# A two-layer-stack transformer kernel: the residual kept feature-major instead of token-major

## The reference

```python
# layers 0 and 1
for i in range(2):
    x = x + 0.5 * swiglu(rmsnorm(x, ffn1_norm[i]), gate[i], up[i], down[i])
    h = rmsnorm(x, mix_norm[i])             # gated linear attention (i=0), latent attention (i=1)
    o_mem = memory_cross_attention(q_mem, rmsnorm(mem, mem_norm[i]), mem_w_kv[i], ...)
    x = x + concat([o, o_mem]) @ w_out[i]
    x = x + 0.5 * swiglu(rmsnorm(x, ffn2_norm[i]), ...)
# layers 2 and 3
for i in range(2):
    h = rms_norm(x, g_mix_pre[i])           # grouped-query attention, and attention into mem_2
    x = x + rms_norm(concat([tok, mo]) @ w_o[i], g_mix_post[i])
    h = rms_norm(x, g_ffn_pre[i])
    x = x + rms_norm((silu(h @ w_gate) * (h @ w_up)) @ w_down, g_ffn_post[i])
```

## Time and profile before

| | |
|---|---|
| median of the runs | 1841.42 us (1838.01 to 1844.0, 3 runs) |
| profiled execution | span 1837.2 us (the page has no time around it) |
| PE | 1718.0 us busy, 94% |
| DVE | 1095.9 us, 60% |
| ACT | 899.6 us, 49% |
| POOL | 76.6 us, 4% |
| moved | 289.20 MB, mean 157 GB/s |
| L1675 to L1677 (gate, up) | 2112 matmuls of 256 columns each |
| L1706 (down) | 3 x 528 of 512 columns |
| L1609 (row products, out and memory too) | 3 x 514 |

### The profile page before, as it was taken

The page is one execution under the profiler, slowest core; times in us unless marked ns, Lnnn a source line. Parts: engine busy times, 40 slices in busy tenths (PEclk is TensorE's granted clock), DMA queues, the critical chain, the costliest instruction groups (busy, mean ns, idle before and its releaser), DMA issues.

```text
span 1837.2 us, 29340 instructions
## 1 busy us (share of the span) xinstructions
PE 1718.0 (94%) x10778; PEld 1516.3 (83%) x10778; DVE 1095.9 (60%) x1613; ACT 899.6 (49%) x1430; POOL 76.6 (4%) x99
## 2 busy tenths in 40 slices
PE   7999999889999999999799999996899998889998
PEld 6999887579999899987678999873699986579997
DVE  4555666455555655567765555558565556755554
ACT  5444453445444544445555444456544444754443
POOL 1000000000000100001201000000100000110000
PEclk9999999999999999999899999999999998999999
DMA  6655444245555455545224555550255553145553
GB/s 210 194 192 183 162 148 138 92 160 161 188 183 187 149 184 185 182 158 184 80 96 155 190 184 186 170 174 1 97 201 193 179 184 107 47 138 190 185 185 114
DMA packets 79654, 289.20 MB, mean 157 GB/s; under 512 B 8928, under 2 KB 9184, under 8 KB 79216
## 3 DMA queue, kind: packets, MB, share of 16 engines
q1 hardware_dynamic: 78272, 282.23, 46.4%
q0 software_dynamic: 1008, 5.24, 0.8%
q10 hardware_dynamic: 320, 1.01, 0.2%
HBM read 287.39 MB, written 1.05 MB: 157 GB/s over the span
## 4 chain that ended last, share of the span: by engine, by line
PE 81%; DVE 9%; ACT 5%; issue 2%; DMA 2%; POOL 1%; SPq 0%; DVEq 0%; ACTq 0%
PE ps L1706 18%; PE ps L1609 16%; PE ps L1677 13%; PE ps L1675 13%; PE ps L1676 13%; DVE wlo L981 2%; PE ps L1555 2%; PE ps L1937 2%; PE ps L1901 1%; DMA raw<-units 1%; ACT whi L637 1%; DVE inv L1476 1%; DVE act_lo L992 1%; ACT junk L660 1%; ACT act_hi L648 1%
## 5 line engine op out<-in xcount | busy, mean ns | idle before, releaser
L1675 PE MATMUL ps<-act_hi,whi 128*128 128x256 f32 x2112 | 603.1, 286 | 4.0 <-DVE wlo L981 3.1
L1676 PE MATMUL ps<-act_lo,whi 128*128 128x256 f32 x2112 | 599.8, 284 | 0.0
L1677 PE MATMUL ps<-act_hi,wlo 128*128 128x256 f32 x2112 | 599.7, 284 | 0.0
L1157 DVE TENSOR_TENSOR wlo<-raw,whi 128x1024 fp32r<-128x1024 f32 x358 | 437.0, 1221 | 177.9 <-ACT whi L777 177.7
L1675 PEld LDWEIGHTS ps<-act_hi,whi 128*128 128x128 f32 x2112 | 407.4, 193 | 10.9 <-DVE wlo L981 3.7
L777 ACT ACTIVATE whi<-raw 128x1024 fp32r<-128x1024 f32 x358 | 365.7, 1052 | 101.9 <-DMA raw<-units 100.9
L1676 PEld LDWEIGHTS ps<-act_lo,whi 128*128 128x128 f32 x2112 | 407.4, 193 | 4.7
L1677 PEld LDWEIGHTS ps<-act_hi,wlo 128*128 128x128 f32 x2112 | 407.2, 193 | 0.0
L981 DVE TENSOR_TENSOR wlo<-raw,whi 128x1024 fp32r<-128x1024 f32 x176 | 211.9, 1226 | 116.0 <-ACT whi L637 115.5
L1126 DVE TENSOR_TENSOR prob<-ps,prob 128x512 f32<-128x512 f32 x132 | 91.3, 692 | 252.8 <-PE ps L1677 252.6
L637 ACT ACTIVATE whi<-raw 128x1024 fp32r<-128x1024 f32 x176 | 180.9, 1055 | 119.2 <-DMA raw<-units 114.1
(11 more groups left out here) (187 smaller groups left out, 1522.2 us busy)
## 6 DMA issues: line engine op xcount, KB each, us to landing
raw<-units SPq DMA_DIRECT2D x534, 512.0 KB, 3.4
arena<-mem_in POOLq DMA_DIRECT2D x3, 1024.0 KB, 6.8
gpost<-post_in POOLq DMA_DIRECT2D x4, 512.0 KB, 4.8
x<-x_in SPq DMA_DIRECT2D x2, 512.0 KB, 4.6
out<-x SPq DMA_DIRECT2D x2, 512.0 KB, 3.2
const<-const_in ACTq DMA_DIRECT2D x1, 816.0 KB, 4.5
row<-row_in ACTq DMA_DIRECT2D x1, 134.0 KB, 5.1
const<-const_in SPq DMA_DIRECT2D x1, 64.0 KB, 3.0
```

What stands on the lines that cost most here:

```text
L1157: V.tensor_tensor(wlo[:, u % RING, :], raw[:, u % RAW, :], whi[:, u % RING, :].bitcast(F32), ALU.subtract).then_inc(lo_ready, 1)
L1675: T.matmul(out_, whi[:, slot, w], act_hi[:, k, :], start=k == 0, stop=False)
L1676: T.matmul(out_, whi[:, slot, w], act_lo[:, k, :], start=False, stop=False)
L1677: ins = T.matmul(out_, wlo[:, slot, w], act_hi[:, k, :], start=False, stop=k == KD - 1)
```

## The change

- `x`, memory and the output lie with features on partitions (8 tiles of 128 features x 256 tokens). The host turns x, mem and mem_2 before and the output after. No transposes of x or of memory are left; those of keys, queries and probabilities stay.
- Down and out (`sum_unit`): the weight tile is stationary and the hidden chunk or the heads move, 256 columns, 8 output tiles x 3 passes per unit. In the last unit each of the four banks is reported when it is done (`sum_done`), and DVE adds it to x at once (`x_ready` now counts banks).
- The order inside an FFN: down is two chunks behind gate/up instead of one. In the first chunk PE runs all high passes of gate and up first (`norm_hi`), then the low ones (`norm_lo`). Banks 6 and 7 hold the first two chunks. `LEAD` is 4.
- Sum of squares: ACT squares x by banks of 128x512 into `sq`; POOL adds them (`folded`, three adds of 512 columns and one of 256) to `fold`, 256 columns; PE multiplies that by a column of ones (`columns_of_fold`), which gives one sum per token; DVE makes the mean, POOL the root, DVE the diagonal (was POOL), PE spreads it, DVE copies it. `columns_of_fold` stands in PE's list after the third unit of an FFN, `spread` after the fourth. At a post end DVE does the adds.
- Beside memory x is multiplied with the root by POOL (`normed`, four of 128x512). At a post end ACT applies the gain from PSUM (`gained`), DVE multiplies by the spread root and adds, bank by bank. `gpost` and its four loads are gone.
- Loads at the start: gain first, x in four parts with unit 0 between them, the identity behind them; memory is loaded in four parts later.

```diff
-RAW, RING, LEAD = 3, 6, 3
+RAW, RING, LEAD = 3, 6, 4
...
+                def folded(self, slot, first=True):
+                    for b in range(BANKS):
+                        pool.wait_ge(square_ready, self.squares + b + 1)
+                        if b > 0:
+                            if b > 1:
+                                pool.wait_ge(pool_step, self.steps)
+                            nc.gpsimd.tensor_tensor(sq[:, 0], sq[:, 0], sq[:, b], ALU.add).then_inc(pool_step, 1)
+                            self.steps += 1
+                    pool.wait_ge(pool_step, self.steps)
+                    nc.gpsimd.tensor_tensor(fold[:, slot, :], sq[:, 0, 0:S], sq[:, 0, S:2 * S], ALU.add
+                                            ).then_inc(fold_ready, 1)
...
+                def bank_squares(self, src, here):
+                    if self.folds:
+                        act.wait_ge(fold_ready, self.folds)
+                    self.folds += 1
+                    for b in range(BANKS):
+                        here(b)
+                        nc.scalar.activation(sq[:, b], src(b), ACT.Square).then_inc(square_ready, 1)
...
+                        for b in range(1, BANKS):
+                            dve.wait_ge(square_ready, self.squares + b + 1)
+                            self.step(V.tensor_tensor(sq[:, 0], sq[:, 0], sq[:, b], ALU.add))
+                        V.tensor_tensor(fold[:, 0, :], sq[:, 0, 0:S], sq[:, 0, S:2 * S], ALU.add
+                                        ).then_inc(fold_ready, 1)
+                        self.mean(end, 5)
+                        self.diagonal(end)
+                        self.spread(5)
+                        for b in range(BANKS):
+                            dve.wait_ge(gained, self.gains_)
+                            self.step(V.tensor_tensor(o, o, doubled(inv_rms), ALU.mult))
+                            V.tensor_tensor(bank_of(x, b), bank_of(x, b), post_x[:, b], ALU.add).then_inc(x_ready, 1)
...
+                def columns_of_fold(self, slot, bank):
+                    pe.wait_ge(fold_ready, self.folds)
+                    for t in range(TT):
+                        ins = T.matmul(ps[:, bank, t:t + 1], fold[:, slot, t * P:(t + 1) * P], ones[:, 0:1],
+                                       start=True, stop=True)
+                    ins.then_inc(cols_done, 1)
...
+                def sum_unit(self, k, slot, hi, lo, first, last):
+                    for b in range(BANKS):
+                        for d in range(2):
+                            w = slice((2 * b + d) * P, (2 * b + d + 1) * P)
+                            o = ps[:, b, d * S:(d + 1) * S]
+                            T.matmul(o, wlo[:, slot, w], hi, start=first and d == 0, stop=False)
+                            T.matmul(o, whi[:, slot, w], hi, start=False, stop=False)
+                            ins = T.matmul(o, whi[:, slot, w], lo, start=False, stop=last and d == 1)
+                        if last and b < BANKS - 1:
+                            ins.then_inc(sum_done, 1)
+                    ins.then_inc(unit_used, 1)
...
+                    first_chunk()
+                    gate(1, U0 + 2, 0)
+                    self.columns_of_fold(0, 5)
+                    up(1, U0 + 3, 0)
+                    self.spread(5)
+                    gate(2, U0 + 4, 0)
+                    up(2, U0 + 5, 0)
+                    down(0, 0, first=True)
+                    pe.wait_ge(inv_ready, self.diags)
+                    gate(3, U0 + 7, 0)
+                    up(3, U0 + 8, 0)
+                    down(1, 0)
+                    with pe.Fori(0, (CH - 4) // 2) as i:
+                        for c in (4, 5):
+                            pe.wait_ge(scaled_ready, i * 2 + (gu + c - 1))
+                            gate(c, U0 + 3 * c - 2, i)
+                            up(c, U0 + 3 * c - 1, i)
+                            down(c - 2, i)
```

More of the change, by code:

```diff
@@ L215, in ffn @@
             down = self.w["w_down_2"][n]
-        for c in range(CH + 1):
+        for c in range(CH + 2):
             if c < CH:
@@ L303, in build @@
         gate_up_rms = prob[:, 2:4]
-        gpost = sb("gpost", [P, D])
+        flat_rows = rows[:].rearrange("p t n -> p (t n)")
+        sq = flat_rows.rearrange("p (b n) -> p b n", b=BANKS)
+        normed = flat_rows.rearrange("p (k s) -> p k s", k=KD)
+        fold = sb("fold", [P, 2, S])
         const = sb("const", [P, CONST_W])
@@ new lines, in chunk, with left @@
+                        nc.scalar.activation(hid_hi[:, c % 2, :], hid[:, c % 2, :], ACT.Copy).then_inc(hid_hi_ready, 1)
+                        for n in (1, 2):
+                            if n in splits:
+                                raise_hi(U0 + 3 * c + 5 + n, i)
+                    def left(c, splits):
+                        return [n for n in splits if U0 + 3 * c + 5 + n < NU]
+                    chunk(0, 0, (1, 2))
+                    for c in range(1, 4):
+                        chunk(c, 0, (0, 1, 2))
+                        if m is not None and c > 1:
+                            self.memory(m, c - 2)
@@ L787, in ffn @@
+                    with act.Fori(0, (CH - 6) // 2) as i:
+                        for c in (4, 5):
+                            chunk(c, i, (0, 1, 2))
+                    chunk(CH - 2, 0, left(CH - 2, (0, 1, 2)))
+                    chunk(CH - 1, 0, left(CH - 1, (0, 1)))
+                    self.u = U0 + 3 * CH + LEAD
                     self.used += 3 * CH
                     self.gu += CH
-                    self.split(1)
-                    if m is not None:
-                        self.turn_memory(m, 1)
@@ L792, in ffn @@
                     self.end(end)
                 def end(self, end):
+                    self.xs += 1
                     if end.startswith(("post", "fpost")):
[L796 to L802 removed]
@@ new lines, in spread, with norm @@
+                def spread(self, bank):
+                    self.spreads += 1
+                    dve.wait_ge(spread_done, self.spreads)
+                    V.tensor_copy(inv_rms, ps[:, bank, 0:S]).then_inc(inv_ready, 1)
+                def norm(self, name, g, k0):
+                    at = GAIN_AT[g] + k0
+                    for k in range(KD):
+                        self.low(x[:, k, :], at + k, k)
+                        if self.u == 0 and k == 3:
+                            self.split(1)
+                    if self.u == 1:
+                        self.split(LEAD - 1)
+                    self.squares += BANKS
@@ L1074, in scale_heads, with norm_beside_memory @@
                     return ins
-                def norm_beside_memory(self, name, g, k, m):
-                    self.scaled(name, x)
-                    self.split(4)
-                    at = GAIN_AT[g] + k
-                    self.take_lo(range(at, at + 4), 0)
-                    self.split(2)
-                    self.take_lo(range(at + 4, at + 8), 4)
-                    self.split(2)
+                def norm_beside_memory(self, name, g, k0, m):
+                    self.squares += BANKS
+                    self.split(2)
+                    self.mean(f"mem{m}", 4)
+                    self.mean(name, 5)
+                    self.split(1)
+                    self.diagonal(name)
+                    self.spread(6)
+                    at = GAIN_AT[g] + k0
+                    for k in range(KD):
+                        self.low(normed[:, k, :], at + k, k)
+                        if k == 3:
+                            self.split(1)
+                    self.split(4)
                     self.projected(8)
@@ L1102, in memory_keys, with memory @@
                     self.take([(kmT[:, h, :], GAIN_AT["memk_norm"] + m if m < 2 else None) for h in range(XH)])
-                def turn_memory(self, m, half):
+                def memory(self, m, half):
+                    if half == 0:
+                        self.squares += BANKS
                     at = memory_gain(m)
-                    if half == 0:
-                        self.take_lo(range(at + 4, at + 8), 8)
-                    else:
-                        self.take_lo(range(at, at + 4), 4)
+                    for k in range(4 * half, 4 * half + 4):
+                        self.low(mem_x[:, k, :], at + k, MEM_SLOT + k)
@@ new lines, in ffn @@
+                    dve.wait_ge(inv_ready, self.spreads)
+                    chunk(0, 0, (1, 2))
+                    for c in range(1, 4):
+                        chunk(c, 0, (0, 1, 2))
+                        if m is not None and c > 1:
+                            self.memory(m, c - 2)
+                    with dve.Fori(0, (CH - 6) // 2) as i:
+                        for c in (4, 5):
+                            chunk(c, i, (0, 1, 2))
+                    chunk(CH - 2, 0, left(CH - 2, (0, 1, 2)))
@@ L1172, in ffn, with summed @@
+                    chunk(CH - 1, 0, left(CH - 1, (0, 1)))
+                    self.u = U0 + 3 * CH + LEAD
                     self.gu += CH
```

(7 more changed lines are left out.)

614 lines of the change are left out of this document (304 added, 310 removed).

## The result

The kernel after takes 1848.75 us in the median of 9 runs (1844.13 to 1853.68), the kernel before 1841.03 us beside it (9 runs). The ratio is 1.0045, with a 95% interval of 1.003 to 1.0059: slower by about 8 us. That is above the 0.3% that I took as the bound of "no change", though the interval begins at that bound. The prediction of 1837 us was wrong: its sum gave a small gain, the measurement shows a small loss. The time lies in the stated range (1813 to 1855), the forecast's own range (1827 to 1847) does not hold it. Against the forecast span of 1832.4 the miss is 15.4 us.

The account below looks back on a forecast made before the run. PE, busy 94% of the span, was taken to bound the kernel, with time lost at seams. The terms summed to -4.8 us: span 1832.4, with 4.2 added 1837 us; range 1813 to 1855, likeliest case 1827 to 1847.

Parts of the forecast that it names:

- term 7: Start of the kernel: 31.2 us lost before the first down unit would become 18.4; -12.5 us (-8 to -16).
- term 5: Half end beside memory, three places: banks free sooner, transposes and two slow clocks go, some waits added; -7.0 us.
- 1. Turned products: Down and out units: 24 matmuls of 256 columns cost 0.14 us more per unit, 172 units; +24.1 us.
- 2 and 9. Half and add ends: Three seams into an FFN: 2.6 to 2.7 us lost instead of 7.4, -14.1; late folds slow the clock, +4.5.
- term 9: Clock: three late folds would be long enough for the clock to fall, 1.6 us each; +4.5 us.
- 3. Post end to an FFN: Two seams from a post end to an FFN: 11.7 us lost instead of 12.6; -1.8 us.
- 4. Last mixer: Post end to the last mixer: later first low part and late fold, +2.5 us; end of the kernel, +4.8.
- 6. Memory's transposes: Three FFNs: two groups of eight transposes of memory go, 0.88 us each; -5.3 us.
- 8. Without effect: Longer unit lead, gpost's loads off the path, DVE and ACT room in steady chunks: 0, lead at most 2 either way.
- A: Rival: the folds come in time and nothing waits for them; -23 us, 1814 us; chance 0.2.
- B: Rival: folds come later, at additions of 1.35 us or more, and the clock falls each time; 1857 us; chance 0.2.
- C: Rival: turned products cost nothing because two passes with the same weights share a load; 1813 us; chance 0.05.

## Why the prediction was wrong, by its steps

Two terms of the sum were mis-sized, and together they make up 15.3 of the 15.4 us: the start (term 7, -12.5, measured -2.1) and the starts beside memory (term 5, -7.0, measured -2.1). The step that turned the sign is in term 7: a row of the chain was taken for the first down unit and was the second. What the other terms missed cancels.

**1. Turned products (+24.1): right.** 8.64 for 8.50 in each steady chunk but the three named above, and 20 us (21 in the span) when only they are turned back.

**2 and 9. Half and add ends (-14.1) with late folds (+4.5): right in sum, by a different split.** With 0.12 of the last matmul off, 409.61 to 431.05 holds six units and 4.0 us lost, against 7.4 before: three times -3.4 is -10.1, where the two terms together said -9.6. The additions take 1.26 to 2.10 us, median 1.30, where I took 1.2. At the seam at 409 three of them and the half-width one take 6.9 us from the first start to the last end, where the sketch had 6.8 from 6.6 to 13.4. The stand is 1.57 for 1.85. The step that the prediction left open, whether DVE waits for POOL too, is answered: it does, and the low parts take 4.30 us for 3.25 and the splits 4.44 for 2.36. The clock fell after exactly three stands, as term 9 had it, but they are 1.57 us long, under the length of 2.00 to 2.18 that the prediction took from the earlier trace rows. So the number of three was right by luck. (The table spreads term 9 over five FFNs; with all of it at these three seams their rows would be forecast at -3.9 together instead of -6.0. They measured -4.5.)

**3. Post end to an FFN (-1.8): nearly right.** 1311.06 to 1340.6 holds 12.1 us lost, forecast 11.7.

**4. Last mixer (+2.5) and end (+4.8): right.** +3.7 and +5.1 by stage, against 3.6 (with 1.1 of term 1) and 4.8. The last store lands 14.3 us after the last matmul's start. The chain there in the kernel after shows the forecast's steps: three additions, column sums, root, diagonal, spread, then a product and a sum per bank on DVE:

```profile
1513.57 0.70 DVE rows L1293
...
1515.02 0.44 DVE fold L1295
...
1515.50 0.62 PE ps L1674 x4
...
1517.65 1.24 PE ps L1682 x2
1518.91 0.44 DVE prob L1122
...
1519.37 0.70 DVE arena L1305
1520.09 0.69 DVE x L1306
...
1524.77 0.41 DVE act_lo L1098
...
1525.27 7.65 PE ps L1718 x24
```

**5. Beside memory (-7.0): mis-sized.** Less the 0.14 of their out units the three mixers came out at -0.1, +1.3 and -3.3, together -2.1. Of that, +1.3 and -2.7 are the stretches of attention named under the table, which were no term of mine. Without them the three starts gave -0.1, 0.0 and -0.6, so even the -2.1 is partly luck. The 3.2 us for two slow clocks that go is the failed item: they do go at the banks' wait (the clock is 1.00 at 804.8 to 810.8), but PE's stand for memory's eviction, for which I had counted 0.5 us more, is 1.2 us longer at both places (2.80 and 3.08 for 1.61 and 1.91), and a new slow stretch (0.72) stands behind it. The experiment on the eviction gives about 4 us back.

**6. Memory's transposes (-5.3): right**, less a new stand of 0.87 us at 1017.81, where memory's additions on POOL stretch DVE's low parts.

**7. Start (-12.5): this step failed.** I read the row at 42.71 as the first down unit. It is the second. The chain shows only the pieces that lie on it, and the first down unit at 32.47 is not among them. PE's timeline of the kernel before has both:

```profile
32.47 0.73 PE L1706 MATMUL ps<-whi,hid_hi 128*128 128x512 f32 x2 [0.67 <-DVE hid_lo L1132]
...
42.71 0.73 PE L1706 MATMUL ps<-whi,hid_hi 128*128 128x512 f32 x2 [0.60 <-DVE hid_lo L1132]
```

So the start had lost 20.9 us, not 31.2. (With 31.2 the prediction's own difference is 12.8, not 12.5.) The new start, which I put at 18.4 us lost, loses 14.4: down begins at 31.7, 4 us better than I said. Most of that is the wait for the fold, 0.99 us at 20.89 instead of 2.5, with the clock at 1.00 behind it (21 to 27) instead of a fall for 1.6. The gain is -6.5, and 5.25 of it go again in the chunk with the stand at 51.75 (13.89 us instead of 8.64), which was no term of mine: I counted memory's transposes as removed, but not that its squares and low parts now wait in DVE's list for a load that POOL issues later. The kernel before issued it whole, and where it works on memory PE stands only 0.76 us, at 41.83. The first FFN, less 3.1 for term 1 and with 1.8 for the transposes, gives -2.1 for the start. That is 10.4 of the 15.4 us between forecast and span; the other 4.9 are term 5. With the row read rightly and all else as it was, the sum would have been +5.4 instead of -4.8, a small loss.

**8. Without effect: right** for the lead and for DVE's and ACT's room in the steady chunks; DVE has 2.4 us to spare in a chunk of 8.64 in the window above, and outside the three distances named above no steady chunk has a hole. Those three lie inside the loop that I had excluded from DVE's and ACT's room: that room was read from a chunk without memory's work. The lead was not tried by itself.

**Rivals.** A (folds in time, 1814) did not occur. The variant with additions on DVE comes close to that case, with PE waiting for no fold in the FFNs, and it saves 15 us where A said 23. B (additions of 1.35 or more, the clock falls each time, 1857) came about by half: the additions average 1.48, and the clock falls at three of the ten places. C is refuted. What the forecast had right in sum it had partly by offsetting errors, and what made the sign wrong was one misread row.

## What to carry to other kernels

Before a mark is taken from a chain of waits, look it up in the engine's own timeline: a chain leaves out work that others overtook, and the "first" of a kind there need not be the first. When a load is issued later, look at what stands in the list of the engine that uses it: all of that now waits for the landing, needed or not. An addition given to an idle engine is not free where the two engines hold each other up; here the kernel was 15 us faster with the same additions on the busier engine.

## What the runs showed that I had not expected

- **DVE waits for POOL as POOL waits for DVE.** Low parts of x took 644 ns each with POOL's additions beside them and 479 without, memory's 794 and 478, two splits 4.44 and 2.36 us. The Trainium skill, "SBUF — State Buffer", section "Who interferes with whom", says that a DVE instruction with two SBUF inputs and a GpSimd one that reads SBUF contend, and that the order of issue decides who is blocked; in these runs both are longer when they overlap: POOL's additions beside DVE's work take up to 2.10 us for 1.26 at the least.
- **DVE is about twice as fast at the same addition**: 690 ns for 128x512 (39 of them), POOL 1262 ns at the least.
- **The clock does not go by the length of a stand alone.** After 1.57 us at 418.25 the mean granted clock was 0.72 over 6 us (PE without a hole for the 6 us before). After 1.58 at 1350.73 in the variant with one more addition it was 1.00, after 1.91 at 1197.11 in the one with the earlier eviction also 1.00, after 2.70 at 428.11 in the variant with one more addition 0.72. What makes the difference is open; no run separated it.
